# An eleventh place of 16 KB for expert weights, filled once per round, in a decoder layer with 32 experts

## The reference

```python
def moe_ffn(h, w_router, b_router, w_exp_in, b_exp_in, w_exp_out, b_exp_out):
    t = h.reshape(B * S, D)
    logits = (t @ w_router + b_router).astype(jnp.float32)
    top_v, top_i = lax.top_k(logits, TOP_K)
    top_w = jax.nn.softmax(top_v, axis=-1)
    combine = jnp.sum(jax.nn.one_hot(top_i, N_EXPERTS, dtype=jnp.float32) * top_w[..., None], axis=1)
    def expert_step(acc, p):
        w1, b1, w2, b2, ce = p
        u = t @ w1 + b1
        g = jnp.minimum(u[:, :D_FF], SWIGLU_LIMIT)
        lin = jnp.clip(u[:, D_FF:], -SWIGLU_LIMIT, SWIGLU_LIMIT)
        a = g * jax.nn.sigmoid(SWIGLU_ALPHA * g) * (lin + 1)
        y = a @ w2 + b2
        return acc + ce[:, None].astype(y.dtype) * y, None
```

## Time and profile before

| | us |
|---|---|
| median of three runs | 1345.77 (1345.77 to 1346.25) |
| the profiled execution: time | 1345.52 |
| the profiled execution: first to last instruction (span) | 1343.6 |
| PE busy | 1307.8 (97%) |
| DVE, ACT, POOL busy | 468.7, 326.1, 26.9 |
| DMA over the span | 475.04 MB, mean 354 GB/s |
| the chain that ended last | PE 86%, DMA 10%, ACT 2%, DVE 2% |
| granted clock of PE | 0.997 |

### The profile page before, as it was taken

One profiled execution on the slowest core, in us unless ns is written; L12 is line 12 of the kernel. 1 busy time (PEld: TensorE's weight loads), 2 busy tenths in 40 slices (PEclk: granted clock), 3 DMA queues, 4 the chain that ended last, 5 costly groups with the idle time before them and its releaser, 6 DMA issues.

```text
span 1343.6 us, 15841 instructions
## 1 busy us (share of the span) xinstructions
PE 1307.8 (97%) x6443; PEld 672.0 (50%) x6443; DVE 468.7 (35%) x800; ACT 326.1 (24%) x481; POOL 26.9 (2%) x40
## 2 busy tenths in 40 slices
PE   9999999999999999999999999999999999999996
PEld 8889888988887333333333333333333333333332
DVE  6753655444566223222232222322223222232223
ACT  5665455564344001110011000100011001011001
POOL 4000000000101000000000000000000000000000
PEclk9999999999999999999999999999999999999998
DMA  9543443537579999999999999999999999999995
GB/s 322 202 176 141 172 175 136 188 126 274 188 262 367 393 429 430 429 433 432 430 430 434 431 431 431 433 430 430 432 432 431 430 433 432 430 430 434 431 430 242
DMA packets 67880, 475.04 MB, mean 354 GB/s; under 512 B 7488, under 2 KB 9600, under 8 KB 43264
## 3 DMA queue, kind: packets, MB, share of 16 engines
q1 hardware_dynamic: 65552, 472.75, 84.9%
q10 hardware_dynamic: 2288, 1.73, 0.4%
HBM read 473.42 MB, written 1.05 MB: 353 GB/s over the span
## 4 chain that ended last, share of the span: by engine, by line
PE 86%; DMA 10%; ACT 2%; DVE 2%; issue 0%; SPq 0%; DVEq 0%; ACTq 0%
PE bank L1646 47%; PE bank L1456 18%; DMA place<-in_w_exp_in 9%; PE bank L1443 8%; PE bank L1760 4%; PE bank L1674 1%; PE bank L1659 1%; ACT fxqT L877 1%; PE bank L1723 1%; PE bank L1699 1%; PE bank L1647 1%; PE bank L1580 1%; PE bank L1599 1%; DVE w_lo L944 0%; DMA ring<-in_w_in 0%
## 5 line engine op out<-in xcount | busy, mean ns | idle before, releaser
L1646 PE MATMUL bank<-place,fxqT 128*64 128x512 f32 x1536 | 687.6, 597 | 20.9 <-ACT fxqT L877 15.1
L1647 PE MATMUL bank<-place,fxqT 128*64 128x512 f32 x1536 | 687.7, 597 | 0.0
L1646 PEld LDWEIGHTS bank<-place,fxqT 128*64 128x64 f32 x1536 | 199.3, 137 | 420.5 <-issue 389.9
L1266 DVE TENSOR_SCALAR big_a<-bank 128x512 f32<-128x512 f32 x32 | 22.1, 692 | 523.8 <-PE bank L1647 523.8
L1647 PEld LDWEIGHTS bank<-place,fxqT 128*64 128x64 f32 x1536 | 199.3, 137 | 0.0
L944 DVE TENSOR_TENSOR w_lo<-ring,w_hi 128x2048 fp32r<-128x2048 f32 x63 | 145.2, 2305 | 141.6 <-ACT w_hi L618 141.4
L618 ACT ACTIVATE w_hi<-ring 128x2048 fp32r<-128x2048 f32 x63 | 120.7, 1915 | 157.1 <-PE bank L1456 109.3
L865 ACT ACTIVATE big_a<-big_a 128x512 f32<-128x512 f32 x32 | 20.2, 630 | 434.0 <-DVE big_a L1266 434.0
L1296 DVE TENSOR_TENSOR xs<-bank,xs 128x512 f32<-128x512 f32 x132 | 81.9, 682 | 35.8 <-PE bank L1760 35.8
L1456 PE MATMUL bank<-w_hi,h_hi 128*128 128x512 f32 x224 | 88.3, 394 | 0.1
L1456 PE MATMUL bank<-w_lo,h_hi 128*128 128x512 f32 x224 | 87.2, 389 | 0.0
(11 more groups left out here) (287 smaller groups left out, 1267.3 us busy)
## 6 DMA issues: line engine op xcount, KB each, us to landing
place<-in_w_exp_in SPq DMA_DIRECT2D x127, 2048.0 KB, 27.8
place<-in_w_exp_out SPq DMA_DIRECT2D x63, 2048.0 KB, 28.2
ring<-in_w_in SPq DMA_DIRECT2D x19, 2048.0 KB, 7.5
ring<-in_w_branch SPq DMA_DIRECT2D x6, 2048.0 KB, 7.6
ring<-in_w_mem_kv SPq DMA_DIRECT2D x4, 2048.0 KB, 7.9
ring<-in_w_out SPq DMA_DIRECT2D x2, 2048.0 KB, 11.0
ring<-in_w_in SPq DMA_DIRECT2D x2, 1024.0 KB, 7.8
place<-in_w_exp_in SPq DMA_DIRECT2D x2, 1024.0 KB, 40.7
```

The costliest lines, as they stand in the source:

```text
L1266: dve.tensor_scalar(gate.rearrange("c (q p) -> c q p", q=4), bank[0][:, :].rearrange("c (p q) -> c q p", q=4), LIMIT, None, ALU.min).then_ ...
L1646: mm(o[0:CAP, :], lhsT, low, start=start, stop=stop)
L1647: return mm(o[CAP:P, :], lhsT, high, start=start, stop=stop)
```

## The change

The places become a ring of ten (`RING_PLACES`) and one more, `SPARE`, in the memory that smaller persistent buffers leave free.

- **Pieces and places.** Pieces 0 to 9 go into places 0 to 9 as before, piece 10 (expert 1's first piece of layer two) goes into the spare place, and from there on piece c goes into ring place (c - 1) % 10. The spare place isn't filled again in the round. The load of piece 10 is issued behind that of place 5, when DVE has drained slot 59.
- **The loop.** Two experts stand ahead of the loop (`HEAD`), the loop of five runs five times, and five experts follow outside.
- **Memory.** `yS`, `sel`, `pick_e` and `row_of` lie over the merged rows, so POOL makes `row_of` only when these have been turned. `b1raw` and `b2raw` lie in the expert part's own buffer `moe_b` and share memory with a buffer of the mixing part, so both are loaded behind slot 60, behind a wait for DVE's drain of slot 59, and both are rounded behind slot 62. `act_out` is `lin`. `selW` lies over the router's weights.
- **`gfin`** lies in place 1 and is loaded by SP behind the last piece.

```diff
-PLACES = 10
+RING_PLACES = 10
+PLACES = RING_PLACES + 1
+SPARE = RING_PLACES
+HEAD = 2
 TURN = 5
+TURNS = (NE - HEAD) // TURN
...
-        moe_b = big_a
+        moe_b = sb("moe_b", [P, 3 * 512])
+        b1raw, b2raw = moe_b[:, 0:D], moe_b[:, D:D + 512]
...
         def piece_turn(r, m, c):
-            b = c % PLACES
-            return b, r * place_uses(b) + m * CYCLE + c // PLACES
+            if m is None:
+                b, used = (c % RING_PLACES, c // RING_PLACES) if c < SPARE else (SPARE, 0)
+                if c > SPARE:
+                    b, used = (c - 1) % RING_PLACES, (c - 1) // RING_PLACES
+            else:
+                c += HEAD * PIECES - 1
+                b, used = c % RING_PLACES, m * CYCLE + c // RING_PLACES
+            return b, r * place_uses(b) + used
...
             load_ahead(5)
+            sp.wait_ge(dve_drained, dve_drains(LAST_B2))
+            load_ahead(SPARE)
...
+            with sp.If(busiest < CAP + 1):
+                sp.wait_ge(place_used[1], place_uses(1))
+                load_final(final_in)
...
+            pool.wait_ge(filled[7], turn(7, ("mg", 3)))
             pool.memset(row_of[:, :, :], 0.0).then_inc(row_step, 1)
...
-                if i == 44:
-                    act.dma_start(gfin[:, :], norm_final.partition_broadcast(P)).then_inc(final_in, 16)
+                if i == 60:
+                    act.wait_ge(dve_drained, dve_drains(LAST_B2))
                     for r in range(4):
                         act.dma_start(b2raw[32 * r:32 * r + 32, :],
                                       b_exp_out[0, :, 512 * (r // 2):512 * (r // 2 + 1)]).then_inc(b2_in, 16)
-                if i == 50:
-                    act.wait_ge(b2_in, 64)
-                    act.activation(b2split[:, :], b2raw[:, :], ACT.Copy).then_inc(b2_rounded, 1)
-                if i == 60:
                     for r in range(4):
                         half = b_exp_in[0].rearrange("e (q h n) -> e q h n", q=2, h=2)[:, :, r // 2, :]
...
                 if i == 62:
+                    act.wait_ge(b2_in, 64)
+                    act.activation(b2split[:, :], b2raw[:, :], ACT.Copy).then_inc(b2_rounded, 1)
                     act.wait_ge(b1_in, 64)
```

More of the change, by code:

```diff
@@ L243, in part @@
             return mixing.enter_context(nc.sbuf_tensor(name, shape, dt))
+        part("rest_a", [P, 2 * (D + 4) - 3 * 512])
+        rows = part("rows", [64, P])
+        wg = part("wg", [P, KT, 16])
+        bF = part("bF", [12, 1])
+        bI = part("bI", [4, 1])
+        mruns = part("mruns", [64, S], F32R)
+        acol = part("acol", [P, TT, 4])
+        floor = part("floor", [P, TT, 4])
+        p_a = part("p_a", [P, 512])
+        den = part("den", [P, TT, 4])
+        rden = part("rden", [P, TT, 4])
+        fac = part("fac", [P, TT, 4])
+        msq = part("msq", [P, TT, 4])
+        fxmask = part("fxmask", [P, 384])
+        cF = part("cF", [12, S])
+        part("rest_spare", [P, 1848])
         ring = [part(f"ring{b}", [P, KT, UW]) for b in range(RING)]
@@ L272, in build @@
         cFs = part("cFs", [64, S], F32R)
-        fxmask = part("fxmask", [P, 384])
-        cF = part("cF", [12, S])
         mixing.close()
-        place = [sb(f"place{b}", [P, KT // 2, 2 * UW]) for b in range(PLACES)]
+        spare = sb("spare", [P, KT // 2, 2 * UW])
+        place = [sb(f"place{b}", [P, KT // 2, 2 * UW]) for b in range(RING_PLACES)] + [spare]
+        gfin = place[1][:, 0, :]
         weights_in = [sem(f"weights_in{b}") for b in range(RING)]
@@ L482, in load_piece, with load_final, load_turns @@
                 sp.wait_ge(place_used[b], used)
-                load(m * TURN + c // PIECES, c % PIECES, b)
-            with sp.Fori(0, NE // TURN - 1) as m:
-                for c in range(PLACES, PLACES + TURN * PIECES):
-                    load_piece(0, m, c)
-            for c in range(PLACES, (TURN + NE % TURN) * PIECES):
-                load_piece(0, NE // TURN - 1, c)
+                load(expert_of(m, c // PIECES), c % PIECES, b)
+            def load_final(loaded):
+                sp.dma_start(gfin, norm_final.partition_broadcast(P)).then_inc(loaded, 16)
+            def load_turns(r):
+                with sp.Fori(0, TURNS - 1) as m:
+                    for c in range(TURN * PIECES):
+                        load_piece(r, m, c)
+                for c in range(TURN * PIECES):
+                    load_piece(r, TURNS - 1, c)
+            for c in range(PLACES, HEAD * PIECES):
+                load_piece(0, None, c)
+            load_turns(0)
             sp.wait_ge(route_ready, 1)
             busiest = sp.value_load(most[0:1, 0:1], min_val=0, max_val=S)
+            with sp.If(busiest < CAP + 1):
+                sp.wait_ge(place_used[1], place_uses(1))
+                load_final(final_in)
             with sp.If(busiest > CAP):
@@ L494, in _ @@
                     with sp.If(busiest > r * CAP):
-                        with sp.Fori(0, NE // TURN) as m:
-                            for c in range(TURN * PIECES):
-                                load_piece(r, m, c)
-                        for c in range(NE % TURN * PIECES):
-                            load_piece(r, NE // TURN, c)
+                        for c in range(HEAD * PIECES):
+                            load_piece(r, None, c)
+                        load_turns(r)
+                sp.wait_ge(moe_end, 1)
+                load_final(final_late_in)
             sp.wait_ge(final_ready, 1)
```

88 lines of the change are left out of this document (41 added, 47 removed).

## The result

| | before | changed |
|---|---|---|
| median (lowest to highest) | 1345.77 us (1345.02 to 1346.25), 5 runs | 1353.01 us (1350.46 to 1357.27), 5 runs |
| ratio to before | | 1.0055 [1.0044, 1.0066] |
| profiled execution | 1345.52 us, span 1343.6 | 1350.46 us, span 1348.2 |

The changed kernel is slower by 0.55%, above the range of the prediction. Two things stand out ahead of any row: the time rose where I had expected it to fall by 1.5 us, and the runs of the changed kernel spread over 7 us where those of before spread over 1.2. The profiled execution was the mildest of its runs, so what follows explains 4.6 us of span; the median is 2.6 us above that.

What follows compares the result with a forecast made beforehand. The stream of weight refills was taken to set the end: profiled 1345.52 us, less 2.6 for the stream, plus 1.1 for the biases, gave 1344.0, plus 0.25 to the median 1344.3 us; range 1342.0 to 1348.3.

Steps and rivals of the forecast that it cites:

- What is B?: Step estimating when the first bias arrives ahead of ACT's squares: took 419.3 us, costing +1.1 us, ends 0 and +7.
- B: Moment at which the first bias has come and ACT can round it; PE waits from 418.2 us on, by B - 418.2.
- the volume count: Estimate of the bias arrival from bytes queued ahead, with the last bias packets behind place 0: 419.3 us.
- rival C: At ACT's wait for b1_in: biases interleaved with 16 KB packets of places 1 and 7 land at 425; +6.8, 1350.0 us; 12%.
- The additional load is hidden: Piece 10's load, issued near 403.3 us, fits DMA time free from 400 to 420 us and a second hole; cost 0.
- The stream stops once: At piece 21, which waits for piece 11's release at 490.31 us: gain of 3.1 to 3.6 us, not 4.86.
- A part of that is lost again: In the refill stream: code fetches delay one DMA engine, 0.5 us, and piece 26's issue 0.1; stream's gain then -2.6 us.
- The rest: Row table, second bias' low part, `gfin`, one loop turn less, release order, PE's instructions: all 0, a few tenths at most.
- A: Refill stream: the full piece is gained, release early enough or nothing lost on a nearly empty queue; 1342.0 us; 6%.
- rival B: At the first bias' arrival: biases cost nothing, landing at 418.2 us or before; 1343.2 us, to 1342.2; 20%.
- D: Refill stream: the lead isn't worth anything, gain 0 to 1 us; 1344.8 to 1346.9 us with the biases; 14%.

Runs made afterwards that it cites:

- experiment 3: Kernel before, with the second bias loaded behind slot 60 and rounded behind slot 62 as in the changed kernel, without the spare place; 1346.91 us, 1.0008.
- experiment 2: Changed kernel with the loads of the spare place and of place 0 cut into eight DMAs each, in 2 KB packets; 1345.01 us, 0.9995.
- experiments 5 and 6: Kernel before with only the loop reshaped: two (5) or seven (6) experts ahead of the loop, five behind it; 1346.83 and 1346.88 us.
- experiment 1: Changed kernel, but SP issues the eight bias loads ahead of the spare place's load, instead of ACT; 1344.18 us, 0.9989.
- Experiment 7: experiment 1 with seven experts ahead of the loop and the additional place used three times, for pieces 10, 21 and 32; 1342.88 us, 0.9981.
- 17 calls: Changed kernel with 17 calls of matmuls on constants, results unread, ahead of the turning of xs in slot 63; 1351.53 us.
- 32 calls: Changed kernel with 32 calls of matmuls on constants, results unread, ahead of the turning of xs in slot 63; 1351.35 us.
- experiment 4: Changed kernel, but SP waits for the first bias to land before issuing the spare place's load; 1345.88 us, 1.0006.

## Why the prediction was wrong, point by point

**The failed step is "What is B?"** The wait that was built on B held. The formula said that PE waits from B = 418.2 on, by B - 418.2: 3.76 for 421.96, and 3.94 was measured; 1.6 for 419.8 in experiment 3, and 1.71 was measured; 0.7 for 418.94 in experiment 2, where it was 0.34. DVE's variance ended with POOL's instruction again, though it took 1.25 us, not 1.51. What failed was the value: I chose the volume count, 419.3, over the turns packet by packet, 425. The turns were right: 78 packets against 78 from 415 to 419 us. By the packets, what kept B below 425 was a pause of q1, and not where I had looked for it, between place 0 and place 1, but ahead of place 0, where 234 small packets went out in 1.5 us. That 422 lies between my two ends is luck: I hadn't worked that pause out. Experiment 2 charges 3.0 us to the 16 KB packets. The rule of the Trainium skill that I cited, in "DMA: Bandwidth & Descriptors", on queues, rings and completion order, would have given 428; the direction agrees with the trace, the size doesn't.

**The term left out is the clock.** I had a wait of PE in the sum and priced it one for one. From 422.2 to 426.2 TensorE did nothing, the granted clock went to 0.5, and the work behind took 2.2 us more. So a 3.9 us wait cost about 6.1. With it rival C's price at B = 422 is +6 instead of +3.8. The Trainium skill's "TensorE: Matmul & The Clock Gate", in its part 1 on the clock gate, says that the gate goes by how busy the array has been of late; by that rule the wait has a price behind it too, and the trace agrees.

**Release of place 0.** Predicted +1.1 (439.9), measured +5.58: +3.9 wait, +2.2 clock, and -0.5 that stays open. Fewer instructions of the second bias among the slots could be a reason, but experiments 5 and 6, which have the mixing part of before, differ by 0.4 in their releases (438.38 and 438.77).

**The additional load is hidden: right.** It landed at 402.81 + 11.1 = 413.9 and the last load ahead at 442.7, ahead of the first refill at 444.36. But I proved only that it costs the stream nothing. Filling the hole took the hole from the biases; the 2.8 us of the earlier trace rows held for an empty queue.

**The stream stops once: right, the size too small.** Predicted -3.1 at piece 21, measured -2.33. The gap of landings was 7.5 us, not 6.6: the issue at 495.96 is within 0.1 us the old refill 12 plus 5.58, the landing took 8.4 us instead of 7.7 and refill 10 came 0.1 earlier, counted from the release. A packet of code started at 500.7, inside that landing, so the 7.5 need not all be the stop; in experiment 1 the gap is 6.9. Experiment 7 confirms the mechanism by removing it.

**"A part of that is lost again": mis-sized.** I took 0.5 + 0.1 with ends 0 and 1.6; from -2.33 at piece 21 it went to -1.1 by piece 32, 1.2 us. The loop's shape goes with that much in the kernel before too (experiments 5 and 6, medians, either interval just including none), though at other pieces, and I had put it at nothing under "The rest". The stream's whole gain was 1.0 us, where I had 2.6.

**PE's waits**: predicted 4.3 us from about 1175 on; they begin at 1153 and hardly shrink: the eight distances of the puts from 1097.55 to 1325.34 add up to 227.8 us, those from 1092.52 to 1320.62 before to 228.1, so 6.9 became 6.6. PE came 5.0 us later to the last experts and the stream 4.6, so there was little to take.

**Rivals.** C is what happened, at its place, ACT's wait, and by its mechanism, the turns, at 12%; but the packets were those of place 0 (landed at 421.75, the last bias at 421.94), not of places 1 and 7, and the landing behind place 1 that I had named as its sign didn't come: B was 422, not 425. By C's own formula 422 costs 3.8 us and leaves the time at 1347; that the profiled execution came out past the 1350.0 of C is the clock and the smaller gain of the stream, and the median holds the spread besides. A fell with the step at piece 21, rival B with the PE wait, and of D the stream's part came about, a gain of 1.0. C got too little because I set a row that shows the turns, 353 packets against 353, below a count of volume that no row showed to hold between two queues.

**The sum as it should have been**, in the profiled execution: 1345.52 + 3.9 + 2.2 - 0.5 - 1.0 = 1350.1; measured 1350.46. The median lies 2.6 us above that, and none of the terms accounts for it. **Open:** why the runs of the changed kernel spread from 1350.5 to 1357.3. The kernel with 17 calls spreads as widely (1348.0 to 1356.7), while experiment 1, without the bias in its way, doesn't (1343.9 to 1345.0), so B is the suspect. The mean granted clock of each run fits a longer wait in the slower ones: with 17 calls it is 0.997 in the three runs up to 1350.1 us and 0.995 to 0.996 in the three from 1353.0 on, as if the wait had outlasted them, and with 32 calls 0.997 to 0.998 in all. But the range of B in the four profiles is 1.8 us, no profile caught an execution of 1355 us, and experiment 4, whose profile has no wait for B, has a run of 1351.83 at a clock of 0.995 too.

## What to carry to other kernels

A transfer that fills idle DMA time is free only for the queue it stands in: list every small transfer that relied on that idle time, find its consumer, and issue it first, since behind and between large packets it waits its turns. A ring that gets one more buffer for one use keeps the lead only until the round in which that buffer drops out; there the refill waits for the next release, so follow the releases one round further before counting the gain. And price an idle stretch of TensorE of some microseconds at more than its length, by what a row of the lower clock shows.

## What the runs showed of the hardware

- Four DMAs of 128 KB on ACT's queue: the page's median from issue to landing was 2.8 us with the other queue empty, 4.7 on SP's queue behind 256 KB, 7.3 beside 2 KB packets, 7.7 beside 16 KB packets. The medians hide the one that counts: the last took 2.8, 4.8, 8.0 and 11.77 us.
- With both queues at work the DMA engines took one packet of each in turn, whatever its size: 78 of 16 KB against 78 of 2 KB in 4 us, 90.3% of the engines' time against 10.6%. In a pause of q1 234 small packets went out in 1.5 us. In experiment 3 there is a stretch of 2.5 us, 60 against 13, that doesn't fit.
- TensorE idle for 3.9 us, then a granted clock of 0.51 over 7 us, in another execution with nearly the same wait 0.76 over the same 7 us: the cost of one wait isn't the same in each run. 34 small matmuls in 3.96 us and a rest of 1.5 us kept it at 1.00, and so did a wait of 1.71 us without them (experiment 3).
- DVE's 128x2 instruction that runs beside POOL ends with POOL's first half in the changed kernel too. POOL's work by tile (duration ns min/median/max, first and last start) puts that at 423.16 + 2.35 = 425.5, and the variance ended at 424.27 + 1.25 = 425.52:

```profile
L615 POOL TENSOR_TENSOR b1split<-moe_b,b1split x2: 2334/2346/2358, 423.2 to 425.6; 32x1024 fp32r<-32x1024 f32 x2
```
